# The end of a convolution's silu in a hybrid layer kernel: one added on ACT, product on GpSimd

## The reference, cut to what matters

```
def causal_dwconv(x, w, b):
    K = w.shape[0]
    S = x.shape[1]
    xp = jnp.pad(x, ((0, 0), (K - 1, 0), (0, 0)))
    y = xp[:, 0:S] * w[0]
    for k in range(1, K):
        y = y + xp[:, k:k + S] * w[k]
    return y + b
...
xbc = jax.nn.silu(causal_dwconv(xbc, ssd_conv_w[layer], ssd_conv_b[layer]))
xs, bm, cm = _split(xbc, (D_INNER, BC_DIM, BC_DIM))
```

## Time and profile before

| | us |
|---|---|
| median of 3 runs | 1028.66 |
| lowest and highest | 1027.56, 1028.87 |
| the profiled execution | 1028.22 |
| its span, first to last instruction | 1026.5 |

### The profile page before, as it was taken

The page is one execution under the profiler, slowest core; times in us unless marked ns, Lnnn a source line. Parts: engine busy times, 40 slices in busy tenths (PEclk is TensorE's granted clock), DMA queues, the critical chain, the costliest instruction groups (busy, mean ns, idle before and its releaser), DMA issues.

```text
span 1026.5 us, 13649 instructions
## 1 busy us (share of the span) xinstructions
PE 1017.6 (99%) x5215; PEld 835.5 (81%) x5215; DVE 640.3 (62%) x901; ACT 462.3 (45%) x826; POOL 88.5 (9%) x128
## 2 busy tenths in 40 slices
PE   9999999999999999999999999999999999999997
PEld 8887777788788888878888888888888888888886
DVE  7646899785475685985854544666666666641332
ACT  6344556555555546665532222544434444331233
POOL 0001001110132120122220100000000000000000
PEclk9999999999999999999999999999999999999999
DMA  7622222225556425445352733123232223232212
GB/s 219 124 85 82 64 80 69 93 68 126 158 147 155 123 72 157 139 112 158 106 192 89 273 131 120 65 82 122 84 122 82 82 89 115 96 129 83 96 69 82
DMA packets 123500, 116.50 MB, mean 113 GB/s; under 512 B 21343, under 2 KB 111783, under 8 KB 123448
## 3 DMA queue, kind: packets, MB, share of 16 engines
q1 hardware_dynamic: 95509, 94.74, 29.7%
q10 hardware_dynamic: 25346, 12.59, 5.2%
q0 software_dynamic: 2592, 8.46, 2.3%
HBM read 109.41 MB, written 6.36 MB: 113 GB/s over the span
## 4 chain that ended last, share of the span: by engine, by line
PE 90%; DVE 7%; ACT 1%; issue 1%; POOL 0%; ACTq 0%; DVEq 0%; POOLq 0%
PE banks L1276 28%; PE banks L1277 27%; PE banks L1278 27%; DVE conv_acc L1224 2%; PE banks L1399 1%; DVE w_lo L870 1%; PE banks L1392 1%; PE banks L1387 1%; PE banks L1351 1%; PE banks L1328 1%; PE banks L1375 1%; PE banks L1338 0%; DVE bc L1229 0%; PE banks L1448 0%; PE banks L1287 0%
## 5 line engine op out<-in xcount | busy, mean ns | idle before, releaser
L870 DVE TENSOR_TENSOR w_lo<-w_raw,w_hi 128x1024 fp32r<-128x1024 f32 (+1 forms) x166 | 200.1, 1246 | 122.3 <-ACT w_hi L585 121.0
L585 ACT ACTIVATE w_hi<-w_raw 128x1024 fp32r<-128x1024 f32 (+1 forms) x166 | 164.1, 1037 | 107.6 <-PE banks L1278 107.6
L1276 PE MATMUL banks<-xn_hi,w_hi 128*128 128x512 f32 x528 | 211.6, 401 | 1.0 <-DVE conv_acc L1224 1.0
L1277 PE MATMUL banks<-xn_lo,w_hi 128*128 128x512 f32 x528 | 206.0, 390 | 0.0
L1278 PE MATMUL banks<-xn_hi,w_lo 128*128 128x512 f32 x528 | 206.0, 390 | 0.0
L1276 PE MATMUL banks<-hn_hi,w_hi 128*128 128x512 f32 (+1 forms) x376 | 141.3, 376 | 0.0
L1277 PE MATMUL banks<-hn_lo,w_hi 128*128 128x512 f32 (+1 forms) x376 | 141.2, 375 | 0.0
L1278 PE MATMUL banks<-hn_hi,w_lo 128*128 128x512 f32 (+1 forms) x376 | 141.2, 375 | 0.0
L1276 PEld LDWEIGHTS banks<-xn_hi,w_hi 128*128 128x128 f32 x528 | 99.2, 188 | 27.0 <-issue 6.0
L1278 PEld LDWEIGHTS banks<-xn_hi,w_lo 128*128 128x128 f32 x528 | 99.1, 188 | 21.5
L1277 PEld LDWEIGHTS banks<-xn_lo,w_hi 128*128 128x128 f32 x528 | 99.3, 188 | 18.9
(11 more groups left out here) (223 smaller groups left out, 1457.3 us busy)
## 6 DMA issues: line engine op xcount, KB each, us to landing
w_raw<-in_w_in SPq DMA_DIRECT2D x29, 1024.0 KB, 5.4
w_raw<-in_w_up SPq DMA_DIRECT2D x22, 1024.0 KB, 5.1
decay<-acs_scratch ACTq DMA_DIRECT2D x16, 512.0 KB, 6.2
w_raw<-in_w_ssd_o SPq DMA_DIRECT2D x8, 1024.0 KB, 5.7
w_raw<-in_w_down SPq DMA_DIRECT2D x8, 1024.0 KB, 5.1
w_raw<-in_w_in SPq DMA_DIRECT2D x16, 256.0 KB, 4.6
w_raw<-in_w_attn_o SPq DMA_DIRECT2D x16, 256.0 KB, 4.6
decay_off<-acs_scratch ACTq DMA_DIRECT2D x32, 128.0 KB, 3.7
```

The costliest lines, as they stand in the source:

```text
L585: A.activation(whi[:, c % 2, lo_:hi_], raw[:, c % 2, lo_:hi_], ACT.Copy).then_inc(w_rounded, 1)
L870: V.tensor_tensor(wlo[:, c % 2, lo_:hi_], raw[:, c % 2, lo_:hi_], f32(whi[:, c % 2, lo_:hi_]), ALU.subtract).then_inc(w_split, 1)
L1276: T.matmul(out_, w[0], m[0], start=first, stop=False)
L1277: T.matmul(out_, w[0], m[1], start=False, stop=False)
```

## The change

For the first sixteen convolutions DVE's instruction at the end is gone. ACT follows its tanh by an Identity with a bias column of ones, in place (cth = cth + 1), after waiting for the tanh through c_tanh; and POOL multiplies cth by cacc into bc or xs after waiting for c_one. For the convolutions 16 to 23 DVE's instruction stays, with one further wait for c_out.

```
+        c_one = sem("conv_tanh_plus_one")
...
+                    if kind == "bc" or kind == "xs" and i < 4:
+                        k = 2 * i + u + (8 if kind == "xs" else 0)
+                        dst = bc[:, 2 * i + u, :] if kind == "bc" else xs[:, 2 * i + u, :]
+                        eng.wait_ge(c_one, k + 1)
+                        eng.tensor_tensor(dst, cth[:, u, :], cacc[:, u, :], ALU.mult).then_inc(c_out, 1)
...
                         A.activation(cth[:, u, :], cacc[:, u, :], ACT.Tanh).then_inc(c_tanh, 1)
+                        if k_conv < 16:
+                            eng.wait_ge(c_tanh, k_conv + 1)
+                            A.activation(cth[:, u, :], cth[:, u, :], ACT.Identity, bias=ones[:, 0:1]).then_inc(c_one, 1)
                         k_conv += 1
...
                         rides(c, u, 1)
-                        eng.wait_ge(c_tanh, k_conv + 1)
-                        dst = bc[:, t - 16, :] if kind == "bc" else xs[:, t, :]
-                        V.scalar_tensor_tensor(out=dst, in0=cth[:, u, :], scalar=1.0, in1=acc,
-                                               op0=ALU.add, op1=ALU.mult).then_inc(c_out, 1)
+                        if k_conv >= 16:
+                            eng.wait_ge(c_out, k_conv)
+                            eng.wait_ge(c_tanh, k_conv + 1)
+                            V.scalar_tensor_tensor(out=xs[:, t, :], in0=cth[:, u, :], scalar=1.0, in1=acc,
+                                                   op0=ALU.add, op1=ALU.mult).then_inc(c_out, 1)
                         k_conv += 1
```

## The result

The changed kernel took 1034.68 us (median of 4 runs, 1034.26 to 1035.3); the kernel before took 1028.76 beside it. The ratio is 1.0059, with a 95% interval of 1.0047 to 1.0072: slower by 0.6%, 5.9 us. The forecast was 1032.1 us, with a range up to 1034.8. The direction was right; the time lies at the upper end of the range, and the loss of 3.7 us was sized 2.2 us too small. The profiled execution took 1034.27 us, with a span of 1032.5.

A forecast was written before the change was run, and what follows sets the result against it. TensorE bounds the kernel, with little slack over the chain of DVE and ACT. ACT's addition net of DVE's relief, 2.26, plus 1.45 for the port gave +3.7 on 1028.4: 1032.1 us, range 1028.4 to 1034.8.

The forecast's parts named there:

- What bounds the kernel: TensorE carries 90% of the chain; its one sizable wait, 1.0 us, is for taps 8 on DVE, at 155.06 us.
- The addition on ACT: An Identity of 0.72 us behind each tanh delays everything behind it on ACT by 0.76 us (0.67 to 0.85).
- The walk: Delays along the DVE and ACT chain: convolutions 1 to 2 0.6, 2 to 3 0.7, 3 to 4 0.76, 4 to 8 0.2.
- the relief wins: Rival, 0.10: ACT's addition hides in its idle time, taps 8 come at least 1.2 us earlier; 1027.5 us.
- nothing moves: Rival, 0.20: port and ACT eat DVE's gain, taps 8 stay within 1.5 us; 1028.2 to 1030.2, centre 1028.7.
- The port: POOL's products stretch DVE operations with two SBUF sources: 0.4 at product 0, 1.05 at product 3, together 1.45 us.
- the upper end: Contention bound of 2.9 us, if tiny DVE sums of the mask step also stop behind products 4 and 6.
- the reading with 1033.5 us: By the skill's rule, DVE and GpSimd block each other for whole instructions; the tiny sums stop too, giving 1033.5 us.
- The forecast's own upper bound: 2.26 for ACT net of relief, 2.85 for contention and 0.5 uncertainty: 5.6 us, or 1034.0 us.
- After 200 us as before, shifted: Nothing added for convolutions 12 to 15 in 200 to 250 us; the kernel then runs as before, shifted.
- The queue on POOL: Rival, 0.06: products and probabilities wait behind each other on POOL, so PE's transposes wait; 1036 us.

The follow-up runs named there:

- kernel without collisions: Changed kernel, but GpSimd's products 0, 3 to 7 and 9 wait until the DVE work they collided with is done; 1030.56 us, ratio 1.002 against the kernel before.
- the product still on DVE: Against the kernel before: ACT adds one after its tanh, DVE does the plain product, no product on POOL; 1034.06 us, ratio 1.0046.
- all but convolution 3: Changed kernel, except that convolution 3 ends on DVE as before, with nothing on ACT or POOL; 1034.07 us, ratio 1.0051 against the kernel before.
- the product on GpSimd alone: Against the kernel before: for convolutions 0 to 15 GpSimd multiplies x by the bare tanh, and nothing is added on ACT; 1031.2 us, ratio 1.0019.

## Why the prediction came out as it did

**What bounds the kernel: right.** PE's slack over DVE and ACT's common chain decides. PE stopped at the two places named (forecast about 128 and 156 us, measured 130.48 less a pause of 2.69, and 160.20 less 2.10), together for 4.8 us (forecast 4 to 5); the second place came 2 us later than named. DVE's busy time in 100 to 150 us is 40.8 (forecast 38 to 41), and its waits name ACT's rounding, exponentials and copy.

**The addition on ACT: right to 0.2 us.** The row of L799 (line, count, busy, mean ns, and the idle time before) has the 0.72 that was taken from the nearest row of before:
```profile
L799 ACT ACTIVATE conv_tanh<-conv_tanh,ones 128x512 f32<-128x512 f32 x16 | 11.6, 724 | 0.5
```
The walk gave 0.6, 0.7, 0.76 and 0.2, and 2.26 at taps 8. The kernel without collisions (the one with the products put beside nothing) gives, step by step, 0.63, 0.63, 0.75 and 0.07 for the four steps behind, 2.08. That the steps of 0.6 and 0.7 alternate was right too. The two rivals, in which the relief wins and in which nothing moves because ACT and the port eat just what DVE gains, both fall: the additions stand in the chain at 1 to 2, 2 to 3, 3 to 4, 5 to 6 and 7 to 8, and cost 3.79 us against a relief of 1.92.

**The port: this is the step that failed, the term that was mis-sized.** It was forecast at 0.4 + 1.05 = 1.45, bounds 0 to 2.9, and measured 3.59. The steps of the changed kernel less those of the kernel without collisions give the price of each collision: 0.53 (product 0 and `a_lo`), 1.10 (product 3 and the split), 1.04 (product 4 and the `TENSOR_SCALAR` of the mask step), 0.25 (5 and the split), 0.63 (6 and the `TENSOR_TENSOR` of the mask step), 0.04 at 7, together 3.59. Three errors of mine make the 2.1 us between:
- The two tiny instructions of the mask step. I had them at 0.9 and 0.5 and left them for the upper end; the prediction gives no reason for it. The trace of before had one of them beside a GpSimd product, at 71.51 us and only for the product's last 0.11, with its usual 0.16, which settles nothing. They cost 1.67 us, three quarters of what was missing. The Trainium skill (SBUF — State Buffer, Who interferes with whom) has the engine that issues second blocked until the first is done, where DVE has two SBUF inputs or, as `tensor_scalar` can, runs in a mode with two ports. That was the reading with 1033.5 us, and the trace agrees (1.20 and 0.79 us instead of 0.17 and 0.16, both ending with the product); that the `TENSOR_SCALAR` was in such a mode isn't shown. The same section exempts reductions, and the 0.69 us at 145.85 agrees. I had given its reading no weight in the sum; it deserved that of the likeliest case.
- The products 5 and 7 beside the splits behind them, 0.3 us together, were not in the sum.
- The length of the product. I took 1.04 us from the probabilities on the same engine:
```profile
L578 POOL TENSOR_TENSOR xs<-conv_tanh,conv_acc 128x512 f32<-128x512 f32 x8 | 10.4, 1297 | 6.1 <-ACT conv_tanh L799 6.0
```
It is 1.30. The probabilities are multiplied by a column that is repeated, this product has two whole tiles. Each stop that lasts to the end of a product is longer by up to 0.26. Against DVE's 0.69 that is 1.9x; the Trainium skill (GPSIMD Engine Reference, 4.1 Engine selection) has about 2x, and the row that I took, 1.5x, was the wrong neighbour.

**The sum.** 2.08 + 3.59 = 5.67 at taps 8 instead of 3.7. The rest to 6.0 is small: +0.2 between 8 and 16, +0.65 at the transfer near 420 us, and 0.53 less at the start of the stretch. The forecast's own upper bound, 5.6 us or 1034.0, was thus passed, by 0.07 at the taps and by 0.7 in the time. It was built of the right parts, and the value inside it was chosen from the wrong side. That the time lies within the stated range is luck: no case of the prediction gives a time between 1034.0 and its end at 1034.8.

**After 200 us as before, shifted: nearly.** The change itself costs 0.2 there. In two of the experiments it is otherwise: with the product still on DVE a third wait came, and where the clock drops behind the last wait (all but convolution 3) the loss is kept.

**The queue on POOL** cost nothing: no transpose waited for probabilities in the changed kernel.

**Left open.** Which pauses of PE cost the clock: in the traces those of 2.69, 2.75, 2.97 and 4.61 us did, and 2.68 in another kernel, 2.35 and less did not. The untraced runs of a kernel differ in their mean clock (0.997 to 1.000 with the product on GpSimd alone, whose traced pause is 1.83), so one trace of each doesn't settle it. And why the transfer near 420 us is late in some executions and not in others wasn't tried.

## What to carry over

Before an instruction is moved from DVE to GpSimd, lay the two timelines over each other and list every DVE instruction with its sources in SBUF that would run beside it, those of 4 elements too; only the reductions weren't held up here. Each costs up to the whole length of the GpSimd instruction, not a share of its own. If the move must be made, choose the moment: a wait on GpSimd's side for the DVE work to be over gave back 3.6 of the taps' 5.7 us here, and no cost showed. And an addition on an engine that is busy half the time costs its full length wherever the other engine of the chain waits for what stands behind it; convolutions 4 and 6, where nothing did, were the only ones tried on which the taps came earlier, 1.07 us, and only with their products put off. In the time of the whole even that is within the noise.

## What the runs showed of the hardware

- An instruction of 128x4 on DVE, 0.17 us long, lasted 1.20 beside a GpSimd product and ended with it to within 0.02 us, as four others did; a reduction of 128x512 and products with one operand in PSUM were not held up (0.69 and 0.68 us).
- GpSimd's `TENSOR_TENSOR` of 128x512 takes 1.30 us with two whole tiles and 1.04 with one tile and a repeated column. Held up itself, between the halves of a split, it took 2.27.
- A pause of 2.7 us of TensorE can be followed, about 1 us after its end, by some 3.5 us at 1.2 GHz, worth 1.6 us. Whether that is paid depends on what follows: in front of another wait it was free (the changed kernel), behind the last one it was not (all but convolution 3).
